# Two inner tiles split ahead of the last up unit, and modulation sums taken as columns, in a two-block transformer kernel

## The reference

```python
# block 1: retention + indexed attention, then a gated feed-forward with a causal convolution
h = h + rms_norm(mixed, mix_norm_post[l])
up = causal_dwconv(rms_norm(h, ffn_norm_pre[l]) @ w_up[l], conv_w[l], conv_b[l])
g, u = jnp.split(up, 2, axis=-1)
h = h + rms_norm((jax.nn.silu(g) * u) @ w_down[l], ffn_norm_post[l])
# block 2: two layers (hgrn2 mixer, then nsa attention), each with a swiglu feed-forward
c_act = jax.nn.silu(c)
mods = jnp.einsum('bd,lde->lbe', c_act, ada_w) + ada_b[:, None, :]      # four times 3 x 1024
kv_shift, kv_scale = jnp.split(c_act @ kv_ada_w + kv_ada_b, 2, axis=-1)
shift, scale, gate = jnp.split(mods[2 * layer], 3, axis=-1)
x = x + gate[:, None, :] * mixer(rms_norm_2(x, gain) * (1 + scale) + shift)
x = x + gate[:, None, :] * swiglu(modulate(x, norm_ffn[layer], shift, scale), w_in, w_out)
```

## Time and profile before

| | us |
|---|---|
| median of 3 runs (2379.84 to 2380.41) | 2380.25 |
| the profiled execution, whole | 2381.53 |
| its span, first to last instruction | 2379.8 |
| TensorE busy (share of the span) | 2143.7 (90%) |
| VectorE busy | 1295.1 (54%) |
| ScalarE busy | 793.7 (33%) |
| GpSimd busy | 125.6 (5%) |
| mean granted clock | 0.945 |

### The profile page before, as it was taken

How to read it: one execution, slowest core, us unless ns; L and a number is a source line. 1 busy time by engine, 2 the same in 40 slices (tenths; PEclk the granted TensorE clock), 3 DMA queues, 4 the chain that set the end, 5 groups by cost and what they waited for, 6 DMA issues and landing times.

```text
span 2379.8 us, 28136 instructions
## 1 busy us (share of the span) xinstructions
PE 2143.7 (90%) x10760; PEld 1734.0 (73%) x10760; DVE 1295.1 (54%) x2205; ACT 793.7 (33%) x1379; POOL 125.6 (5%) x100
## 2 busy tenths in 40 slices
PE   3998896999898799999899999799579988999997
PEld 3876575888787688887787878679456657888786
DVE  2479447788653524673655564564576854222334
ACT  2333434333323435122422222333246533222221
POOL 0002301000000110000000000100201100000000
PEclk8999898999999899999999999899689879999999
DMA  4321123556342132102456553223200122233221
GB/s 145 107 71 54 36 72 97 185 172 200 116 164 84 62 105 91 36 1 71 145 165 206 166 180 121 80 76 106 73 1 2 37 95 78 93 97 98 89 97 45
DMA packets 146641, 233.08 MB, mean 98 GB/s; under 512 B 7276, under 2 KB 83532, under 8 KB 146252
## 3 DMA queue, kind: packets, MB, share of 16 engines
q1 hardware_dynamic: 142304, 222.28, 28.7%
q10 hardware_dynamic: 3340, 5.85, 0.7%
q0 software_dynamic: 864, 3.15, 0.4%
HBM read 229.16 MB, written 2.10 MB: 97 GB/s over the span
## 4 chain that ended last, share of the span: by engine, by line
PE 80%; DVE 11%; issue 3%; ACT 3%; POOL 2%; DMA 1%; ACTq 0%; DVEq 0%; POOLq 0%
PE ps L1919 10%; PE ps L1921 10%; PE ps L1920 10%; PE ps L1941 5%; PE ps L1942 4%; PE ps L1943 4%; PE ps L1888 4%; PE ps L2176 4%; PE ps L1889 4%; PE ps L1890 4%; PE ps L2093 4%; PE ps L2095 3%; PE ps L1958 3%; PE ps L1983 2%; PE ps L1970 2%
## 5 line engine op out<-in xcount | busy, mean ns | idle before, releaser
L1348 DVE TENSOR_TENSOR w_lo<-ring,w_hi 128x1024 fp32r<-128x1024 f32 (+4 forms) x362 | 376.3, 1042 | 785.9 <-ACT w_hi L882 784.9
L882 ACT ACTIVATE w_hi<-ring 128x1024 fp32r<-128x1024 f32 (+4 forms) x362 | 329.3, 912 | 978.9 <-PE ps L1921 460.4
L1919 PE MATMUL ps<-x_hi,w_hi 128*128 128x512 f32 x1056 | 415.1, 393 | 0.3 <-DVE w_lo L1348 0.3
L1920 PE MATMUL ps<-x_lo,w_hi 128*128 128x512 f32 x1056 | 411.0, 389 | 0.0
L1921 PE MATMUL ps<-x_hi,w_lo 128*128 128x512 f32 x1056 | 411.0, 389 | 0.0
L1919 PEld LDWEIGHTS ps<-x_hi,w_hi 128*128 128x128 f32 x1056 | 198.2, 188 | 50.6 <-DVE w_lo L1348 8.7
L1920 PEld LDWEIGHTS ps<-x_lo,w_hi 128*128 128x128 f32 x1056 | 198.3, 188 | 42.0 <-issue 1.4
L1921 PEld LDWEIGHTS ps<-x_hi,w_lo 128*128 128x128 f32 x1056 | 198.2, 188 | 41.7
L1941 PE MATMUL ps<-w_hi,x_hi 128*128 128x512 f32 x528 | 207.7, 393 | 15.6 <-DVE x_hi L1408 15.6
L1942 PE MATMUL ps<-w_lo,x_hi 128*128 128x512 f32 x528 | 206.8, 392 | 0.0
L1943 PE MATMUL ps<-w_hi,x_hi 128*128 128x512 f32 x528 | 206.7, 391 | 0.0
(11 more groups left out here) (291 smaller groups left out, 3181.9 us busy)
## 6 DMA issues: line engine op xcount, KB each, us to landing
ring<-in_ada_w SPq DMA_DIRECT2D x48, 1024.0 KB, 5.1
ring<-in_ffn_w_in SPq DMA_DIRECT2D x88, 512.0 KB, 4.8
ring<-in_w_up SPq DMA_DIRECT2D x44, 512.0 KB, 4.5
ring<-in_ffn_w_out SPq DMA_DIRECT2D x20, 1024.0 KB, 4.9
ring<-in_hgrn_w_in SPq DMA_DIRECT2D x16, 1024.0 KB, 5.2
ring<-in_w_in SPq DMA_DIRECT2D x12, 1024.0 KB, 5.0
ring<-in_w_down SPq DMA_DIRECT2D x10, 1024.0 KB, 4.9
ring<-in_kv_ada_w SPq DMA_DIRECT2D x8, 1024.0 KB, 5.1
```

Source lines behind the costliest of these rows:

```text
L882: a.activation(to[:, n % depth, 0:src.shape[-1]], src, ACT.Copy).then_inc(s["hi_done"], 1)
L1348: v.tensor_tensor(to[:, n % depth, 0:width], src, hi[:, n % depth, 0:width].bitcast(F32), ALU.subtract).then_inc(s["lo_done"], 1)
L1919: mm(bs[j], wh[:, k, c], x_hi[:, 2 * q + k], start=first, stop=False)
L1920: mm(bs[j], wh[:, k, c], x_lo[:, 2 * q + k], start=False, stop=False)
```

## The change

**Early tiles.** The high and low halves of inner tiles 0 and 1 get a place of their own, `hid_early`, in the memory of the four `ftmp` tiles that the last up unit doesn't use. ScalarE and VectorE split the first down weight piece and these two tiles beside the last up unit (before the last unit's results are taken out). The second down weight piece is split between the taps and the products of the last unit. Tiles from 2 on are split as before.

**Columns.** For j < 4 TensorE now takes 128 columns of the accumulator as weights and one column of ones as the moving operand, four times (`ada_sums`), so that the sums come out as four columns; VectorE adds the bias to them (`ada_column`) and for a scale applies the gain (`ada_gain`). Gates stay rows.

**Order of the modulations.** The first feed-forward's up half has 10 as before, its down half now (2,0) and (2,1) in place of the gates (1,4) and (1,5), which move to the first two up units of the second feed-forward. That has 10 in its up half and four, (3,0) to (3,3), in its down half. (3,4) and (3,5) lie in the first two up units of the third. The sums of a down half are held in four `ftmp` tiles and turned into columns together behind it, in one bank (`ada_columns`). None is left beside or behind the third attention.

```diff
-        ADA = [(0, j) for j in range(6)] + [(1, j) for j in range(6)] + [(2, j) for j in range(6)] \
-            + [(4, j) for j in range(4)] + [(3, j) for j in range(6)]
+        ADA = [(0, j) for j in range(6)] + [(1, j) for j in range(4)] + [(2, j) for j in range(2)] \
+            + [(1, 4), (1, 5)] + [(2, j) for j in range(2, 6)] + [(4, j) for j in range(4)] + [(3, j) for j in range(6)]
         ADA_N = {mj: n for n, mj in enumerate(ADA)}
         ada_after = {(0, u): [ADA[u]] for u in range(10)}
-        ada_after.update({(1, u): [ADA[12 + u]] for u in range(11)})
-        ada_down = {0: ADA[10:12], 1: ADA[23:25]}
-        ADA_LATE = ADA[25:]
+        ada_after.update({(1, u): [ADA[12 + u]] for u in range(10)})
+        ada_after.update({(2, u): [ADA[26 + u]] for u in range(2)})
+        ada_down = {0: ADA[10:12], 1: ADA[22:26]}
+        ADA_ROWS = [mj for mj in ADA if mj not in ada_down[0] + ada_down[1]]
...
-            for mj in ada_down.get(i, []):
-                plan_bank(("ada",) + mj)
+            if i in ada_down:
+                plan_bank(("ada_columns", i))
...
-        hid_hi = x_hi[:, 0:4, :]
-        hid_lo = x_hi[:, 4:8, :]
+        hid_early = over("hid_early", [P, 4, S], KT * S + 17408)
+
+        def hid_parts(k):
+
+            if k < 2:
+                return hid_early[:, k], hid_early[:, 2 + k]
+            return x_hi[:, k % 4], x_hi[:, 4 + k % 4]
+
+        def ada_held(m, j):
+
+            for i, held in ada_down.items():
+                if (m, j) in held:
+                    return ftmp[:, (2, 3, 0, 1)[held.index((m, j))]]
+            return ada_acc[:, ADA_ROWS.index((m, j)) % 2]
...
-                up_out(i, FFN_UNITS - 1)
+                w = arrived(act, ("down", i, 0), (0,))
+                high(("down", i, 0), in_halves(w, 2, PIECE)[:, 0, 0])
+                for k in range(2):
+                    hid_ready(act, i, 2 * FFN_UNITS - 3)
+                    a.activation(hid_parts(k)[0], hid[:, k], ACT.Copy).then_inc(s["hid_hi"], 1)
+                up_first(i, FFN_UNITS - 1)
+                high(("down", i, 1), in_halves(w, 2, PIECE)[:, 0, 1])
+                up_silu(i, FFN_UNITS - 1)
                 for g, (k0, n) in enumerate(down_groups):
                     w = arrived(act, ("down", i, g), (0,))
                     for k in range(k0, k0 + n):
                         if k == k0 + n // 2:
                             arrived(act, ("down", i, g), (1,))
                         high(("down", i, k), in_halves(w, n // 2, PIECE)[:, (k - k0) // (n // 2), (k - k0) % (n // 2)])
+                        if k < 2:
+                            continue
                         hid_ready(act, i, k)
-                        if k == 0:
+                        if k == 2:
                             filled(act, ("up", i, FFN_UNITS - 1, 3))
-                        if k >= 4:
+                        if k >= 6:
                             piece_read(act, split_at[("down", i, k - 4)])
-                        a.activation(hid_hi[:, k % 4], hid[:, k], ACT.Copy).then_inc(s["hid_hi"], 1)
+                        a.activation(hid_parts(k)[0], hid[:, k], ACT.Copy).then_inc(s["hid_hi"], 1)
...
-                acc = ada_acc[:, n % 2]
+                acc = ada_held(m, j)
                 if k == 0:
-                    if n >= 2:
-                        filled(dve, ("ada",) + ADA[n - 2])
+                    if n >= 2 and (m, j) in ADA_ROWS and ADA_ROWS.index((m, j)) >= 2:
+                        filled(dve, ("ada",) + ADA_ROWS[ADA_ROWS.index((m, j)) - 2])
...
+                ada_column(m, j, p[:, 0:4], free(("ada", m, j)))
+                evacuated(dve, ("ada", m, j))
+                ada_gain(m, j)
+
+            def ada_columns(i):
+
+                p = filled(dve, ("ada_columns", i))
                 after()
-                prod = junk2.rearrange("p (k n) -> p k n", k=4)
-                step(v.tensor_tensor(prod, p.rearrange("p (k n) -> p k n", k=4), bcast(ident.unsqueeze(1), [P, 4, P]), ALU.mult))
+                for n, (m, j) in enumerate(ada_down[i]):
+                    ada_column(m, j, p[:, 4 * n:4 * n + 4], free(("ada_columns", i)) if n + 1 == len(ada_down[i]) else None)
+                evacuated(dve, ("ada_columns", i))
                 after()
-                raw_col = stat[:, 224 + 4 * (j % 2):228 + 4 * (j % 2)]
-                v.tensor_reduce(raw_col, prod, AX, ALU.add).then_inc(free(("ada", m, j)), 1)
-                evacuated(dve, ("ada", m, j))
-                dst = mod[:, m, 1, 4 * j:4 * j + 4] if j < 2 else raw_col
-                step(v.tensor_tensor(dst, raw_col, vec[:, BIAS + 24 * m + 4 * j:BIAS + 24 * m + 4 * j + 4], ALU.add))
-                after()
+                for m, j in ada_down[i]:
+                    ada_gain(m, j)
+
+            def ada_column(m, j, p, done):
+
+                dst = mod[:, m, 1, 4 * j:4 * j + 4] if j < 2 else mod[:, m, 0, 4 * (j - 2):4 * (j - 1)]
+                ins = v.tensor_tensor(dst, p, vec[:, BIAS + 24 * m + 4 * j:BIAS + 24 * m + 4 * j + 4], ALU.add)
+                if done is None:
+                    step(ins)
+                else:
+                    ins.then_inc(done, 1)
+
+            def ada_gain(m, j):
+
                 if j >= 2:
+                    raw_col = mod[:, m, 0, 4 * (j - 2):4 * (j - 1)]
...
-                up_out(i, FFN_UNITS - 1)
+                w = arrived(dve, ("down", i, 0), (0,))
+                low(("down", i, 0), in_halves(w, 2, PIECE)[:, 0, 0])
+                for k in range(2):
+                    hid_low(i, k)
+                up_taps(i, FFN_UNITS - 1, (0, 1, 2, 3))
+                low(("down", i, 1), in_halves(w, 2, PIECE)[:, 0, 1])
+                up_gated(i, FFN_UNITS - 1)
...
-                        dve.wait_ge(s["hid_hi"], FT * i + k + 1)
-                        v.tensor_tensor(hid_lo[:, k % 4], hid[:, k], hid_hi[:, k % 4].bitcast(F32), ALU.subtract)\
-                            .then_inc(s["x_split"], 1)
+                        if k >= 2:
+                            hid_low(i, k)
                     for mj in ada_down.get(i, [])[g:g + 1]:
                         ada_sum(*mj)
+
+            def hid_low(i, k):
+
+                dve.wait_ge(s["hid_hi"], FT * i + k + 1)
+                hi, lo = hid_parts(k)
+                v.tensor_tensor(lo, hid[:, k], hi.bitcast(F32), ALU.subtract).then_inc(s["x_split"], 1)
...
             post_norm(1, 1, yf, down_keys(0))
-            for mj in ada_down[0]:
-                ada_out(*mj)
+            ada_columns(0)
...
-            def late_terms(i):
-
-                n, k = divmod(i - 96, KT)
-                if 0 <= n < 2:
-                    ada_term(*ADA_LATE[n], k)
-
-            attention("nsa", late_terms, nsa_finish)
-            ada_out(*ADA_LATE[0])
-            ada_sum(*ADA_LATE[2])
-            ada_out(*ADA_LATE[1])
-            ada_out(*ADA_LATE[2])
+            attention("nsa", lambda i: None, nsa_finish)
...
-                mm(b, ones[:, :], ada_acc[:, ADA_N[(m, j)] % 2], start=True, stop=True).then_inc(full(("ada", m, j)), 1)
+                if j < 4:
+                    ada_sums(m, j, b).then_inc(full(("ada", m, j)), 1)
+                else:
+                    mm(b, ones[:, :], ada_held(m, j), start=True, stop=True).then_inc(full(("ada", m, j)), 1)
+
+            def ada_sums(m, j, b, at=0):
+
+                for k in range(4):
+                    ins = mm(b[:, at + k:at + k + 1], ada_held(m, j)[:, k * P:(k + 1) * P], ones[:, 0:1], start=True, stop=True)
+                return ins
...
-                for mj in ada_down.get(i, []):
-                    ada_row(*mj)
+                if i in ada_down:
+                    b = open_bank(("ada_columns", i))
+                    for n, mj in enumerate(ada_down[i]):
+                        pe.wait_ge(s["acc_done"], ADA_N[mj] + 1)
+                        ins = ada_sums(*mj, b, 4 * n)
+                    ins.then_inc(full(("ada_columns", i)), 1)
...
-            for mj in ADA_LATE:
-                ada_row(*mj)
```

13 lines of the change are left out of this document (5 added, 8 removed).

## The result

The changed kernel takes 2355.01 us (median of 4 runs, 2353.02 to 2356.47). The kernel before took 2380.05 us beside it (4 runs, 2377.16 to 2380.41). The ratio is 0.9897 with an interval of 0.988 to 0.9914, so it is faster by 25.0 us. The prediction was 2355.7.

The account below looks back on a forecast made before the run. TensorE was taken to carry the chain almost everywhere, with gains only where it stops. Terms of -0.5 -3.6 -13.8 -8.9 -1.0 +1.2 +2.0 +0 gave -24.6: 2356.9 profiled, median 2355.7; range 2349 to 2370, about 0.8.

Parts of the forecast that it names:

- The borders: Stops between up and down half of the three feed-forwards: -1.0, -2.2, +1.2, and +1.5 for the clock; together -0.5 us.
- the 1.5: Behind the third feed-forward's stop, grown from 2.7 to 3.9 us: slower TensorE clock, +1.5 us (bounds 0 and 2.4).
- the first two inner tiles: Early high and low halves at the three up-to-down stops, counted with VectorE's new order: -0.5 us together, clock included.
- The columns' own term: Fourteen sums between up units as eight one-column instructions, 0.9 us against 1.0 for a row: 0 in total.
- After the first feed-forward: No gate row awaited; the next norm's reciprocal starts at 784.25 in place of 787.89, right behind ScalarE's root: -3.6 us.
- The third attention: Last four 128-key groups without 16 VectorE terms, clock holding: 6.2 us each, 24.8 in place of 38.6, so -13.8.
- The first of the rivals: Clock drops to 1.2 GHz in the 128-key groups even without terms: -2.8 in place of -13.8, 2366.7 us; chance 0.27.
- Behind it: After the third attention: transposes start right behind GpSimd's last addition, -8.9 us, and run shorter, -1.0 (bounds 0 and -1.9).
- Sums in the second down half: Two more sums in the second feed-forward's down half delay weight pieces: 0.6 us each, +1.2 (bounds 0 and 1.8).
- Rows in the third up half: Two modulation rows moved into the third feed-forward's up half, where TensorE has no gap: 1.0 us each, +2.0.
- both column rivals: Sums between up units: cheap, 0.3 us each, 2345.9, chance 0.06; dear, 4 us each, 2397.7, chance 0.05.
- banks are not what TensorE waits for: Rival: TensorE goes straight on at the three up-to-down borders, 19.5 us gained in place of 0.5: 2336.7; chance 0.05.

Follow-up runs that it names:

- the eight terms in the first group: Changed kernel plus eight 128x512 VectorE operations on SBUF data in the first 128-key group of the third attention: 2364.39 us, ratio 0.9931.
- the small operations: Changed kernel plus sixteen VectorE operations of 128x128 on SBUF data in the last 128-key groups: 2367.66 us, ratio 0.9947.
- its borders put back: Changed kernel with early place, early splits and VectorE's new queue order between up and down halves undone: 2351.67 us, ratio 0.9876.

## Why the prediction was right, and where it was not

The forecast of 2355.7 came true to 0.7 us, and its mechanisms were named in advance. But the sum is better than its terms. Between the profiled executions it was 2.4 us short (24.6 against 27.0): 3.3 too little for the third attention and 1.5 of work that nothing touched, against 0.6, 0.8 and 1.1 too little cost or too much gain in the first down half, the transposes and the third up half. The medians then lie 2 us closer than the profiled pair. That 0.7 is left is luck.

- **The borders.** The size was right (-0.74, -2.2, +1.25 and 1.56 of slow clock, against -1.0, -2.2, +1.2, +1.5), and so was the reason for the stop: the eighth bank, which comes through VectorE's queue, shown by reordering that queue and by opening the banks late. The reason for the 1.5 was not: I took it from the longer stop at the third border (3.9 us, nearer to 4.52 than to 2.68). With the stop back at 2.68 the last stretch is as long (133.68 against 133.70), so that term came true by luck; what brings the clock down there stays open. Wrong, too, was the bookkeeping. The step counted the shorter stops under "the first two inner tiles" as one package. Undone alone, the early split proves to be a loss of about 3 us, and the gain is the columns' (1.4 us at the first border, 2.3 at the second) and the new order's (0.8 at the second). The columns' own term stood at 0. The step did say of the second border that two pairs of 128x512 operations were gone, and of the first that VectorE's queue was the stop and not the split; I did not draw from it that the columns had an effect off TensorE.
- **Behind the first down matmul** 0.6 of the first border's gain is given back in a longer slow stretch (clock 0.67 in 639 to 649 against 0.75 in 640 to 650 before). No term stood for that.
- **After the first feed-forward.** The reciprocal was to start at 784.25 and starts at 784.14; the stretch is shorter by 3.55 (3.6 predicted).
- **The third attention.** The term mis-sized: -17.1 in place of -13.8. The four groups took 22.8, not 24.8, since 6.2 as the middle of two bounds was too high for three of them (5.5). The tail that drains the last group gave another 1.35 and had no term. The mechanism, a clock brought down around a stop for the terms, is borne out by the eight terms in the first group, after which in the profiled execution groups without any last 8.94 at a clock of 0.50, and by the small operations, which bring the clock down one group later. That the stop itself does it is not shown apart from the rest: behind a stop of 0.99 us the clock held, and where sums were made three times over it fell without any stop. The first of the rivals, that the clock falls all the same, did not come.
- **Behind it.** The start of the transposes is right (-8.89). Their length is not: -0.24 in place of -1.0, well within the bounds given (0 and -1.9). TensorE stood 2.12 us for the addition, and the 32 transposes started from a low clock as before (0.71 in 1909 to 1914, 0.63 in 1941.5 to 1947 before).
- **Sums in the second down half.** +1.06 in place of +1.2, three of the stops being 0.35 and one 0.38.
- **Rows in the third up half.** Each takes 1.02. The stretch is longer by 3.06; 1.26 of it is the norm's transposes, 6.56 us in place of 5.30 for the same 32, again the clock.
- **Columns.** 0.95 for a sum, as 0.11 an instruction had it; both column rivals are out. The Trainium skill (TensorE: Matmul & The Clock Gate, section "Wait — 56ns, not 53.3ns?") gives about 25 ns as the least distance between starts. The rows show 0.111 us for each of these fp32 instructions, four times that, and tripling their number confirms it.
- **What no term foresaw** is unchanged work at another clock: -1.47 between the second feed-forward and the 128-key groups. TensorE in two windows of the kernel before, and in two of the changed kernel:

```profile
1540.00:1560.00 20.00, 15.07 (x62) 0.84 0.09 24
1560.00:1580.00 20.00, 20.00 (x83) 0.92 0.24 83
```

```profile
1540.00:1560.00 20.00, 16.36 (x71) 1.00 0.17 55
...
1760.00:1765.00 5.00, 4.42 (x28) 0.83 0.01 3
```

The same projections, some 5 us earlier in the changed kernel, run at 0.84 and 0.92 in the one and at 1.00 in the other, which gave some 3 us, and in the first 512-key group the clock fell in the changed kernel alone, which took 1.4 back. Such shifts are why the profiled pair lies 27.0 apart and the medians 25.0.

The rival "banks are not what TensorE waits for" was rightly refused. Its figure, 2336.7, was that of a kernel in which TensorE goes straight on, and the kernel that opens its banks one by one, and nearly does, took 2336.95.

What stays open: what keeps the clock at 1.2 GHz in the 128-key groups while TensorE never idles, and lets it rise after two terms but not after eight. The Trainium skill (the same page, section "Part 4: PE-mode transpose") says that transposes don't count as busy in the same way. These groups are in part transposes, so the low clock that persists is what that rule would lead one to expect; the 32 transposes alone speak against it: the first projection matmul behind them is fast (0.47), and TensorE's clock is 0.50 in 1908.9 to 1910.5 and 1.00 in 1912 to 1914, where it does nothing but transposes. No run here separates the two.

Open, too, is what GpSimd's addition has to do with the stops in these groups, and why the same stop of 2.68 us leaves the clock up in the kernel before and not in the one with its borders put back.

## What to carry to other kernels

When an engine waits for several things at once, find the one that comes last and the one right behind it before an edit is priced: here the early split cost 3 us without the late opening of banks, late opening gave nothing without the early split, and the two gave 15 together. Wait for a buffer where it is first used and not for all of them at the start, and in a shared in-order queue (VectorE's, or the DMA issues) put what frees buffers ahead of what is only needed later. In a stretch of short instructions, count what an added operation on another engine costs when it makes TensorE stop: the stop itself was 1.6 us, the slow clock behind it up to some 10 in the worst execution. And look at the whole stretch behind a stop, not at its first matmul, before you call the clock high.

## What the runs showed of the hardware that I had not expected

- In the 128-key groups with eight terms ahead TensorE was busy for 18.00 of 18.00 us at a granted clock of 0.50 and the clock did not rise; with two terms in place of eight it rose after 3 us. In four executions of one and the same kernel the time varied over 10 us (2357.57 to 2367.75), against 2 to 6 us for the other kernels.
- Stops of the same length end with either clock: behind 2.68 us at the third border it was 1.00 in the kernel before and 0.57 with the borders put back. And the first matmul does not tell it: with the late modulations put back it is 0.47 long behind 3.90 us, and those from the sixth on are 0.63 long.
- The clock also fell with TensorE busy all the time: to a mean of 0.74 in 505 to 510, behind 24 one-column instructions.
- A VectorE operation of a term's form takes 1.55 us beside GpSimd's addition and 0.74 without it, in four kernels out of four.
- Operations of a quarter of the size are hardly cheaper beside these groups: 128x128 takes 0.34 us where 128x512 takes 0.74, and 16 of the small ones, 7.1 us of VectorE with the two long ones, cost the kernel 12.7, where eight of the full size, 6.5 us, cost 9.4 at the median.
